# Final sum of the mixture of experts moved to TensorE, with accumulating stores onto a bias filled in early

## The chip, the cores and the metric

The kernel runs on one core of a Trainium2 chip. The metric is device time in microseconds (us). A profiled execution also has a span, from the first to the last recorded activity on the core, and its own time, which is a little more.

## What is computed

One step of a decoder layer for 512 prompt tokens and 32 sample tokens, 544 rows of width 1024, everything in 32-bit floats. An mLSTM branch and a pooling branch are mixed and projected, a layer norm follows, and then a mixture of experts (16 experts, two per token) and a second layer norm. The change is in the last line of this:

```python
gate = jnp.sum(jax.nn.one_hot(idx, N_EXPERTS) * wts[..., None], axis=1)       # two gates per token
h = jax.nn.silu(xt @ w_e_gate[e]) * (xt @ w_e_up[e]) * gate[:, e]             # for each expert e
x = LN(ALPHA * x + sum_e h_e @ w_e_down[e], ln2_g, ln2_b)                     # y = (s - mean) * rstd * g + b
```

The kernel computes each expert's output without its gate for the tokens routed to it. The last part applies the gates: s = ALPHA * x + gate_a * ya + gate_b * yb, with ya and yb the outputs of a token's two experts.

## The kernel before

All work is written out by hand for each engine, as one instruction stream each, with semaphores between them. The 544 rows are five tiles, four of 128 rows and one of 32 (`ROWS`). The stages are: transposing x, four heads of the mLSTM (h = 0 to 3) beside the wide projections, pooling, mixing, `w_out` with the first layer norm, the router, 16 experts, and the tail that this change is about.

**Loads.** Weights come as 1 MB chunks into three slots of `raw`, all issued by SyncE (SP) in one queue. `load_chunk(c)` waits until VectorE's subtraction (L431) has split the chunk that last used the slot. ScalarE makes the high part (L412) of a chunk and VectorE the low part (L431), since products are made as three float32r matmuls (L436 to L438). For each head h, SP loads the chunks 3h + 8 to 3h + 10, stores the head's states, waits for the store, and loads the state of the next head (`load_state`, L467).

**Second layer norm's parameters.** After the router's rows are stored, SP loads `ln2_g` into `lng` (L582) and `ln2_b` into `lnb` (L583), each broadcast to 128 partitions.

**Experts.** Expert outputs go from PSUM to `ys` (L985 by ScalarE, L1567 by VectorE) and by DMA to `y_slots` in HBM, 512 KB for each expert (L675 by GpSimd, the last one by SP at L598).

**The tail.** GpSimd (POOL) gathers each token's two expert rows from `y_slots` by indirect DMA (L713): five gathers into `ya` once the outputs of the experts before the last have landed, then five into `ybk` once the last has. `x1` already holds ALPHA * x (L973, ScalarE, during the experts). VectorE does the rest: `combine(i, 0)` (L1662) adds gate_a * ya for each tile; then for each tile `combine(i, 1)` (L1662 again) adds gate_b * yb, `stats` makes mean and variance (two L1674, L1676, L1677), `normal` subtracts the mean and multiplies with `lng` (L1681), and a last instruction multiplies with the reciprocal deviation and adds `lnb` (L1688). The combine of tile i + 1 stands between L1681 and L1688 of tile i, while GpSimd computes variance ** -0.5 (L726). SP stores each tile when L1688 has finished (L613). TensorE and ScalarE have nothing to do in the tail.

Of the kernel before, what the change touches and what calls it, by code (L numbers as in the profile page):

```python
# [5 lines left out]
ALU = mybir.AluOpType  # L6
ACT = mybir.ActivationFunctionType
F32 = mybir.dt.float32
# [7 lines left out]
P = 128  # L16
DM = 1024
SEQ, DB, DT = 512, 8, 4
NS = DB * DT
N = SEQ + NS  # L20
PT = SEQ // P
NT = PT + 1
# [11 lines left out]
ROWS = [P] * PT + [NS]  # L34
# [79 lines left out]
def build(nc, consts, x_prompt, x_sample, state_C, state_n, state_m, state_pool, w_in, b_gate, hn_gain, w_pool,  # L114
# [6 lines left out]
    def sem(name):  # L121
        sems[name] = ctx.enter_context(nc.semaphore(name))
        return sems[name]
# [30 lines left out]
    def lay(start, end, *items):  # L154

        out = []
        for name, shape, dt in items:
            out.append(place(name, shape, dt, start))
            start += size(shape, dt)
        assert start <= end, (items[-1][0], start - end)  # L160
        return out
# [28 lines left out]
    hmv = keep("hmv", [P, NT, 2])  # L190
    hve = keep("hve", [P, NT])
    hrs = keep("hrs", [P, NT])
# [4 lines left out]
    lst = keep("lst", [P, NT, 2, 6])  # L197
# [10 lines left out]
    end = cursor[0]  # L208
    assert end <= limit, (end - limit)
    r_moe = r1 + 31744  # L210
# [40 lines left out]
    x1, lng, lnb = lay(r_xt, XT_END, ("x1", [P, NT, DM], F32), ("lng", [P, DM], F32), ("lnb", [P, DM], F32))  # L251
# [36 lines left out]
    ya_rows = place("ya_rows", [P, PT, DM], F32, at_hi)  # L288
    ya_last = place("ya_last", [P, DM], F32, at_lo)
    ya = [ya_rows[:, i, :] for i in range(PT)] + [ya_last[:]]  # L290
    (ybk,) = lay(r_moe, end, ("ybk", [P, NT, DM], F32))
    yb_ = [ybk[:, i, :] for i in range(NT)]

    psum = ctx.enter_context(nc.psum_tensor("psum", [P, 8, 512], F32))
# [5 lines left out]
    def startup(i):  # L300

        return psum[:, 2 * (i % 4):2 * (i % 4) + 2, :]

    def narrow(j):
        return psum[:, 4 + j % 2, :]

    def halves(j):
# [3 lines left out]
    id_in, cst_in, par_in, gate_in, wg_in, nn_in, spn_in, wp_in, x1in, ln_in, wr_in = (  # L311
        sem(n) for n in (
            "id_in", "cst_in", "par_in", "gate_in", "wg_in", "nn_in", "spn_in", "wp_in", "x1in", "ln_in", "wr_in"))
# [3 lines left out]
    c_in, c_out, cp_out, outs, m_out, n_out, pool_out = (  # L317
        sem(n) for n in ("c_in", "c_out", "cp_out", "outs", "m_out", "n_out", "pool_out"))
# [30 lines left out]
    ya_in = [sem(f"ya_in{i}") for i in range(NT)]  # L349
    yb_in = [sem(f"yb_in{i}") for i in range(NT)]  # L350
    xal_ok, dve_tail = sem("xal_ok"), sem("dve_tail")
    fin_ok, v2_ok, r2_ok = (sem(n) for n in ("fin_ok", "v2_ok", "r2_ok"))


    def z_room(eng, j):
# [97 lines left out]
    def _(sp):  # L453
# [10 lines left out]
        def load_state(h):  # L464
            for dt in range(2):
                src = state_C[0][:, h, dt * P:(dt + 1) * P, :].rearrange("b p e -> p b e")
                sp.dma_start(cb[:, :, dt, 0:DH], src).then_inc(c_in, 16)  # L467
# [37 lines left out]
        for h in range(H):  # L505
            dense_chunk(3 * h + 8)
            if h == 0:
                with nc.allow_non_contiguous_dma(reason="one number for each head and sequence"):
                    sp.wait_ge(rows_dve, 1)
                    sp.dma_start(m_prompt[0].rearrange("o h -> h o"), mout[:, DB:DB + 1]).then_inc(m_out, 16)  # L510
                    sp.dma_start(m_sample[0].rearrange("b h -> h b"), mout[:, 0:DB]).then_inc(m_out, 16)
            store_prompt_state(h)
            dense_chunk(3 * h + 9)
            dense_chunk(3 * h + 10)
            if h < H - 1:
                store_sample_state(h)
                sp.wait_ge(c_out, 32 * h + 32)
                load_state(h + 1)
        sp.wait_ge(t_done, T_HEAD + 4 * T_PER_HEAD - 1)
        sp.dma_start(spn[:], state_pool[0].rearrange("b j c -> (b j) c")).then_inc(spn_in, 16)  # L520
        sp.dma_start(wp[:], w_pool[0].rearrange("g c e -> c g e")).then_inc(wp_in, 16)
# [58 lines left out]
        store_rows()  # L580
        sp.wait_ge(x1_out, 16 * NT)
        sp.dma_start(lng[:], ln2_g[0].partition_broadcast(P)).then_inc(ln_in, 16)  # L582
        sp.dma_start(lnb[:], ln2_b[0].partition_broadcast(P)).then_inc(ln_in, 16)  # L583
        sp.wait_ge(g_in[0], 16)
        with sp.Fori(1, NE - 1) as e:
            for j, (wt, half) in enumerate(((w_e_up, 0), (w_e_up, 1), (w_e_down, 0), (w_e_down, 1),
# [19 lines left out]
                    expert_chunk(m, 6 * j + (C_MOE + 96 + m - 6 + 1), wt, e, half)  # L606
            sp.nop()
        sp.nop()
        for i in range(NT):
            r = ROWS[i]  # L610
            sp.wait_ge(fin_ok, i + 1)
            dst = y_prompt[0, i * P:(i + 1) * P, :] if i < PT else y_sample.rearrange("b t d -> (b t) d")
            sp.dma_start(dst, x1[0:r, i, :]).then_inc(outs, 16)  # L613

        sp.wait_ge(outs, 16 * NT)
        sp.wait_ge(pool_out, 32)
        sp.wait_ge(n_out, 64)
# [6 lines left out]
    def _(pl):  # L624
# [85 lines left out]
        def gather_rows(a, buf, i):  # L710
            r = ROWS[i]
            idx = bass.IndirectOffsetOnAxis(ap=dest_i[0:r, a, i:i + 1].bitcast(U32), axis=0)
            pl.indirect_dma_start(buf[i][0:r], None, y_slots, idx).then_inc((ya_in, yb_in)[a][i], 16)  # L713
# [6 lines left out]
        pl.wait_ge(last_out, 16)  # L720
        for i in range(NT):
            gather_rows(1, yb_, i)
        for i in range(NT):
            r = ROWS[i]
            pl.wait_ge(v2_ok, i + 1)
            nc.gpsimd.tensor_tensor(hrs[0:r, i:i + 1], hve[0:r, i:i + 1], minus_half[0:r, 0:1],  # L726
                                    ALU.pow).then_inc(r2_ok, 1)


    @block.scalar  # L730
    def _(ac):
# [300 lines left out]
        with ac.If(extra > 0):  # L1032
# [11 lines left out]
                store_half(0)  # L1044
            ac.nop()
        ac.nop()


    @block.vector
    def _(ve_):  # L1050
# [605 lines left out]
        def step2(ins):  # L1656
            ve_.wait_ge(dve_tail, tail.mark(ins))

        def combine(i, a):
            r = ROWS[i]  # L1660
            ve_.wait_ge((ya_in, yb_in)[a][i], 16)
            return v.scalar_tensor_tensor(x1[0:r, i, :], (ya, yb_)[a][i][0:r], gates_ab[0:r, a, i:i + 1], x1[0:r, i, :],  # L1662
                                          ALU.mult, ALU.add)

        for i in range(NT):
            ve_.wait_ge(xal_ok, i + 1)
            last = combine(i, 0)
        step2(last)
        ve_.wait_ge(ln_in, 64)

        def stats(i):
            r = ROWS[i]
            for q in range(2):
                last = v.bn_stats(lst[0:r, i, q, :], x1[0:r, i, 512 * q:512 * q + 512])  # L1674
            step2(last)
            step2(v.bn_aggr(hmv[0:r, i, :], lst[0:r, i].rearrange("p q s -> p (q s)")))  # L1676
            v.tensor_scalar(hve[0:r, i:i + 1], hmv[0:r, i, 1:2], EPS, None, ALU.add).then_inc(v2_ok, 1)  # L1677

        def normal(i):
            r = ROWS[i]  # L1680
            last = v.scalar_tensor_tensor(x1[0:r, i, :], x1[0:r, i, :], hmv[0:r, i, 0:1], lng[0:r, :], ALU.subtract,  # L1681
                                          ALU.mult)
            if i < NT - 1:
                tail.mark(last)
                last = combine(i + 1, 1)
            step2(last)
            ve_.wait_ge(r2_ok, i + 1)
            v.scalar_tensor_tensor(x1[0:r, i, :], x1[0:r, i, :], hrs[0:r, i:i + 1], lnb[0:r, :], ALU.mult, ALU.add  # L1688
                                   ).then_inc(fin_ok, 1)

        step2(combine(0, 1))
        for i in range(NT):
            stats(i)
            normal(i)


    @block.tensor
    def _(pe):
# [485 lines left out]
            pe.nop()  # L2184
        pe.nop()


# [1 line left out]
_INS = ["x_prompt", "x_sample", "state_C", "state_n", "state_m", "state_pool", "w_in", "b_gate", "hn_gain", "w_pool",  # L2189
# [53 lines left out]
```

## Time and profile before

| | us |
|---|---|
| median of 3 runs | 968.62 (968.04 to 969.16) |
| the profiled execution's own time | 969.72 |
| its span | 968.3 |
| TensorE busy | 876.2 (90%) |
| VectorE busy | 599.3 (62%) |
| ScalarE busy | 385.6 (40%) |
| GpSimd busy | 92.5 (10%) |

Busy time of TensorE counts overlapping matmuls as one stretch, with modelled ends. The page also names the chain of work that ended last; for a change in the last 40 us only the end of that chain, in order of time, tells what is worth something.

### The profile page before, as it was taken

How to read it: one execution, taken by the hardware profiler on the slowest of the kernel's cores; microseconds unless marked ns; L12 is line 12 of the kernel's file. 1: busy time of each engine (PE TensorE's matmuls, PEld its weight loads, DVE VectorE, ACT ScalarE, POOL GpSimd, SP SyncE). 2: the span in 40 equal slices, each digit the busy share in tenths (PEclk: the TensorE clock that was granted, in tenths of full speed). 3: DMA queues.
4: the chain of work that ended last, by engine and by line, in shares of the span. 5: the costliest groups of instructions: out<-in, count | busy, mean ns of one | idle time of the engine just before them, and what ended most of it. 6: DMA issues, size and time to landing. Idle time of an engine off the chain costs nothing.

```text
span 968.3 us, 14553 instructions
## 1 busy us (share of the span) xinstructions
PE 876.2 (90%) x5981; PEld 790.2 (82%) x5981; DVE 599.3 (62%) x826; ACT 385.6 (40%) x401; POOL 92.5 (10%) x81
## 2 busy tenths in 40 slices
PE   6999999999999998999999998498889999999920
PEld 6989889888888987999999997377678888888810
DVE  4634453634646373132332455799999999999958
ACT  3522121141321332322222103466567777777600
POOL 3000000000000000101001011202111111110052
PEclk9989999999999999999999998599999999999975
DMA  9761161360533414223212831589799999999462
GB/s 286 237 239 45 55 217 45 98 218 18 190 110 106 145 56 133 79 65 113 92 62 72 327 123 53 194 307 346 298 372 412 420 415 407 414 413 390 197 228 92
DMA packets 79680, 195.78 MB, mean 202 GB/s; under 512 B 3906, under 2 KB 56858, under 8 KB 67337
## 3 DMA queue, kind: packets, MB, share of 16 engines
q1 hardware_dynamic: 72456, 169.40, 48.4%
q0 software_dynamic: 7168, 25.58, 6.9%
q8 instruction: 43, 0.70, 0.3%
q14 instruction: 13, 0.10, 0.0%
HBM read 167.65 MB, written 27.31 MB: 201 GB/s over the span
## 4 chain that ended last, share of the span: by engine, by line
PE 81%; DVE 11%; DMA 3%; ACT 3%; issue 1%; SPq 0%; POOL 0%; DVEq 0%
PE psum L436 24%; PE psum L438 23%; PE psum L437 23%; DVE split_lo L1395 3%; PE psum L1826 2%; PE psum L1845 2%; PE psum L1836 1%; DVE onehot L1490 1%; DVE last_lo L1395 1%; DMA xg<-x_rows,idx_i 1%; PE psum L2071 1%; PE psum L1874 1%; ACT split_hi L412 1%; PE psum L2025 1%; DMA xn<-in_x_prompt_dram 1%
## 5 line engine op out<-in xcount | busy, mean ns | idle before, releaser
L436 PE MATMUL psum<-x_hi,split_lo 128*128 128x272 f32 x704 | 211.0, 300 | 12.5 <-ACT ht L820 8.3
L437 PE MATMUL psum<-x_lo,split_hi 128*128 128x272 f32 x704 | 203.8, 289 | 0.0
L438 PE MATMUL psum<-x_hi,split_hi 128*128 128x272 f32 x704 | 203.7, 289 | 0.0
L1395 DVE TENSOR_TENSOR split_lo<-raw,split_hi 128x2048 fp32r<-128x2048 f32 x72 | 163.3, 2287 | 11.9 <-ACT split_hi L951 10.2
L431 DVE TENSOR_TENSOR split_lo<-raw,split_hi 128x2048 fp32r<-128x2048 f32 x35 | 80.1, 2290 | 128.5 <-ACT split_hi L412 128.4
L951 ACT CAST split_hi<-raw 128x2048 fp32r<-128x2048 f32 x72 | 137.7, 1914 | 53.3 <-PE psum L438 48.1
L436 PEld LDWEIGHTS psum<-x_hi,split_lo 128*128 128x128 f32 x704 | 134.3, 191 | 17.6 <-ACT ht L820 9.3
L437 PEld LDWEIGHTS psum<-x_lo,split_hi 128*128 128x128 f32 x704 | 134.5, 191 | 1.5 <-issue 1.0
L438 PEld LDWEIGHTS psum<-x_hi,split_hi 128*128 128x128 f32 x704 | 134.2, 191 | 0.0
L436 PE MATMUL psum<-split_hi,xgl 128*128 128x512 f32 x188 | 76.3, 406 | 0.5 <-DVE xgl L1551 0.5
L438 PE MATMUL psum<-split_hi,xgh 128*128 128x512 f32 x188 | 74.4, 396 | 0.0
L437 PE MATMUL psum<-split_lo,xgh 128*128 128x512 f32 x188 | 74.4, 396 | 0.0
L412 ACT CAST split_hi<-raw 128x2048 fp32r<-128x2048 f32 x35 | 66.7, 1905 | 3.9 <-DMA raw<-in_w_in_dram 3.9
L1395 DVE TENSOR_TENSOR last_lo<-raw,last_hi 128x2048 fp32r<-128x2048 f32 x24 | 54.9, 2287 | 4.5 <-ACT last_hi L951 4.5
L951 ACT CAST last_hi<-raw 128x2048 fp32r<-128x2048 f32 x24 | 45.8, 1909 | 12.9 <-PE psum L438 12.9
L436 PE MATMUL psum<-split_hi,x_lo 128*128 128x256 f32 x160 | 47.3, 295 | 0.0
L438 PE MATMUL psum<-split_hi,x_hi 128*128 128x256 f32 x160 | 45.7, 286 | 0.0
L437 PE MATMUL psum<-split_lo,x_hi 128*128 128x256 f32 x160 | 45.7, 285 | 0.0
L669 POOL DMA_INDIRECT xg<-x_rows,idx_i x16 | 31.0, 1937 | 131.1 <-PE psum L2071 80.3
L438 PEld LDWEIGHTS psum<-split_hi,xgh 128*128 128x128 f32 x188 | 36.0, 192 | 7.9
L436 PEld LDWEIGHTS psum<-split_hi,xgl 128*128 128x128 f32 x188 | 36.1, 192 | 7.8 <-issue 0.7
L437 PEld LDWEIGHTS psum<-split_lo,xgh 128*128 128x128 f32 x188 | 36.2, 193 | 7.2
(373 smaller groups left out, 1758.9 us busy)
## 6 DMA issues: line engine op xcount, KB each, us to landing
raw<-in_w_e_gate_dram SPq DMA_DIRECT2D x32, 1024.0 KB, 8.3
raw<-in_w_e_up_dram SPq DMA_DIRECT2D x32, 1024.0 KB, 7.9
raw<-in_w_e_down_dram SPq DMA_DIRECT2D x32, 1024.0 KB, 7.6
raw<-in_w_in_dram SPq DMA_DIRECT2D x26, 1024.0 KB, 6.0
cb<-in_state_C_dram SPq DMA_DIRECT2D x8, 1024.0 KB, 8.2
out_dram<-cb SPq DMA_DIRECT2D x8, 1024.0 KB, 6.2
y_slots<-ys POOLq DMA_DIRECT2D x15, 512.0 KB, 8.0
y_slots<-x_hi POOLq DMA_DIRECT2D x2, 2048.0 KB, 12.1
```

Source lines behind the costliest of these rows:

```text
L412: nc.scalar.copy(split_hi[:, c % SPLIT_SLOTS, :], raw[:, c % RAW_SLOTS, :]).then_inc(w_hi, 1)
L431: nc.vector.tensor_tensor(split_lo[:, slot, :], raw[:, c % RAW_SLOTS, :], split_hi[:, slot, :].bitcast(F32), ALU.subtract).then_inc(w_lo, 1)
L436: nc.tensor.matmul(out, a_lo, b_hi, start=first, stop=False)
L437: nc.tensor.matmul(out, a_hi, b_lo, start=False, stop=False)
L438: return nc.tensor.matmul(out, a_hi, b_hi, start=False, stop=last)
L669: pl.indirect_dma_start(xg[e % 2][:], None, x1_rows, idx).then_inc(g_in[e % 2], 16)
L951: nc.scalar.copy(hi, raw2[:, n % MOE_SLOTS, :]).then_inc(w_hi, 1)
L1395: v.tensor_tensor(lo, raw2[:, n % MOE_SLOTS, :], hi.bitcast(F32), ALU.subtract).then_inc(w_lo, 1)
L1490: last = v.tensor_tensor(onehot[:, i, 0:e1 - e0], bc(const("slot"), 1, [P, e1 - e0, P]), bc(tmp_r[:, i, e0:e1], 2, [P, e1 - e0, P]), ALU.i ...
L1826: last = mm(narrow(j)[:, 0:SEQ - i * P], kt[:, c, i * P:i * P + P], qt[:, c, i * P:SEQ], start=c == 0, stop=c == 1)
L1836: last = mm(psum[:, state_bank(c), 0:VW], kw[:, i, whole(c)], ve[:, i, :], start=i == 0, stop=i == PT - 1)
L1845: last = mm(narrow(j)[:, 0:VW], pb[:, at:at + P], ve[:, i, :], start=i == 0, stop=i == t)
```

## The change

The second combine, VectorE's last instruction per tile and SP's store are replaced.

- ScalarE, after its last expert output, writes five 128x128 diagonal matrices with gate_b on the diagonal (`diag`, placed behind `ybk`).
- TensorE adds into PSUM, two banks for each tile: identity times `x1` (`sum_start`, when gate_a * ya has been added to it) and diagonal times `ybk` (`sum_end`, when the gather has landed). Each is two plain float32 matmuls of 512 columns, 20 in all. The order is: starts of tiles 0 to 3, ends of tiles 0 to 3, start and end of tile 4, which uses the banks of tile 0.
- VectorE keeps the first combine, takes the statistics from PSUM, and writes (sum - mean) * `lng` to `x1` (`centred`). It no longer waits for GpSimd's power. Order: stats(0), centred(0), stats(1), centred(1), ...
- ScalarE multiplies `x1` with the reciprocal deviation, one activation per tile.
- GpSimd, after each power, waits for that activation and issues the tile's store itself, as a DMA that adds to what is in HBM.
- What it adds to is `ln2_b`: SP fills the whole outputs with it, five HBM-to-HBM DMAs with a broadcast source, behind `load_state(2)` in head 1. `ln2_b` is no longer loaded into `lnb`.

```diff
@@ sync engine, in the loop over heads
+            if h == 1:
+                for i in range(PT):
+                    sp.dma_start(y_prompt[0, i * P:(i + 1) * P, :], ln2_b[0].partition_broadcast(P)).then_inc(bias_out, 16)
+                sp.dma_start(y_sample.rearrange("b t d -> (b t) d"), ln2_b[0].partition_broadcast(NS)
+                             ).then_inc(bias_out, 16)
@@
-        sp.dma_start(lnb[:], ln2_b[0].partition_broadcast(P)).then_inc(ln_in, 16)
@@
-        for i in range(NT):
-            r = ROWS[i]
-            sp.wait_ge(fin_ok, i + 1)
-            dst = y_prompt[0, i * P:(i + 1) * P, :] if i < PT else y_sample.rearrange("b t d -> (b t) d")
-            sp.dma_start(dst, x1[0:r, i, :]).then_inc(outs, 16)
@@ gpsimd
+        pl.wait_ge(bias_out, 16 * NT)
         for i in range(NT):
             r = ROWS[i]
             pl.wait_ge(v2_ok, i + 1)
             nc.gpsimd.tensor_tensor(hrs[0:r, i:i + 1], hve[0:r, i:i + 1], minus_half[0:r, 0:1],
                                     ALU.pow).then_inc(r2_ok, 1)
+            pl.wait_ge(n2_ok, i + 1)
+            dst = y_prompt[0, i * P:(i + 1) * P, :] if i < PT else y_sample.rearrange("b t d -> (b t) d")
+            pl.dma_start(dst, x1[0:r, i, :], accum_op=ALU.add).then_inc(outs, 16)
@@ scalar
+        for i in range(NT):
+            r = ROWS[i]
+            nc.scalar.activation(diag[0:r, i, 0:r], const("ident", r)[:, 0:r], ACT.Copy, scale=gates_ab[0:r, 1, i:i + 1]
+                                 ).then_inc(dg_ok, 1)
+        for i in range(NT):
+            r = ROWS[i]
+            ac.wait_ge(pf_ok, i + 1)
+            ac.wait_ge(r2_ok, i + 1)
+            nc.scalar.activation(x1[0:r, i, :], x1[0:r, i, :], ACT.Copy, scale=hrs[0:r, i:i + 1]).then_inc(n2_ok, 1)
@@ vector
         def stats(i):
             r = ROWS[i]
+            ve_.wait_ge(pc_ok, i + 1)
             for q in range(2):
-                last = v.bn_stats(lst[0:r, i, q, :], x1[0:r, i, 512 * q:512 * q + 512])
+                last = v.bn_stats(lst[0:r, i, q, :], summed(i)[0:r, q, :])
@@
+        def centred(i):
+            r = ROWS[i]
+            v.scalar_tensor_tensor(x1[0:r, i, :], summed(i)[0:r].rearrange("p b n -> p (b n)"), hmv[0:r, i, 0:1],
+                                   lng[0:r, :], ALU.subtract, ALU.mult).then_inc(pf_ok, 1)
+
+        stats(0)
+        for i in range(NT):
+            centred(i)
             if i < NT - 1:
-                tail.mark(last)
-                last = combine(i + 1, 1)
-            step2(last)
-            ve_.wait_ge(r2_ok, i + 1)
-            v.scalar_tensor_tensor(x1[0:r, i, :], x1[0:r, i, :], hrs[0:r, i:i + 1], lnb[0:r, :], ALU.mult, ALU.add
-                                   ).then_inc(fin_ok, 1)
+                stats(i + 1)
@@ tensor
+        def sum_start(i):
+            r = ROWS[i]
+            pe.wait_ge(xa2_ok, i + 1)
+            if i >= PT:
+                pe.wait_ge(pf_ok, i - PT + 1)
+            for q in range(2):
+                mm(summed(i)[0:r, q, :], ident[0:r, 0:r], x1[0:r, i, q * 512:q * 512 + 512], start=True, stop=False)
+
+        def sum_end(i):
+            r = ROWS[i]
+            pe.wait_ge(dg_ok, i + 1)
+            pe.wait_ge(yb_in[i], 16)
+            for q in range(2):
+                last = mm(summed(i)[0:r, q, :], diag[0:r, i, 0:r], yb_[i][0:r, q * 512:q * 512 + 512], start=False,
+                          stop=True)
+            last.then_inc(pc_ok, 1)
+
+        pe.wait_ge(dg_ok, 1)
+        for i in range(PT):
+            sum_start(i)
+        for i in range(PT):
+            sum_end(i)
+        sum_start(PT)
+        sum_end(PT)
```

## Rows read from the trace of the kernel before

**Rows 1.** Page, chain that ended last, shares of the span by engine.
```profile
PE 81%; DVE 11%; DMA 3%; ACT 3%; issue 1%; SPq 0%; POOL 0%; DVEq 0%
```
**Rows 2.** Chain of waits, the end: start us, length us, what.
```profile
927.21 6.72 DMA y_slots<-ys
...
934.18 4.71 DMA ybk<-y_slots,dest_i
...
939.01 1.30 DVE x L1662
...
945.76 1.21 DVE lst L1674 x2
...
947.39 1.19 DVE x L1681
948.58 1.21 DVE x L1662
...
951.10 1.21 DVE lst L1674 x2
...
965.05 1.27 DVE x L1688
```
**Rows 3.** One line's answer, last line: the stores of L613.
```profile
DMA to landing us min/median/max: 1.9/2.6/2.6
```
**Rows 4.** Instructions in order of time, tail: start us, length us, engine, line, operation.
```profile
926.44 0.59 ACT L985 COPY ys<-psum 128x512 f32<-128x512 f32 x1 [6.55 <-PE psum L438]
...
927.76 1.28 DVE L1662 SCALAR_TENSOR_TENSOR x<-ya_rows,gates_ab,x 128x1024 f32<-128x1024 f32 x1 [0.63 <-DMA ya_rows<-y_slots,dest_i]
...
930.97 2.58 DVE L1662 SCALAR_TENSOR_TENSOR x<-ya_rows,gates_ab,x 128x1024 f32<-128x1024 f32 x2 [1.92 <-DMA ya_rows<-y_slots,dest_i]
...
934.81 1.29 DVE L1662 SCALAR_TENSOR_TENSOR x<-ya_rows,gates_ab,x 128x1024 f32<-128x1024 f32 x1 [1.27 <-DMA ya_rows<-y_slots,dest_i]
```
**Rows 5.** Chain of waits, head 0: plain float32 matmuls, 128x512 (two matmuls are four records).
```profile
79.65 1.91 PE psum L1826 x4
```
**Rows 6.** Stretches: us, busy us (count) by engine, PEclk, DMA share, GB/s.
```profile
622.00:623.00 1.00, 0.79 (x2) 0.70 (x3) 1.00 (x1) 0.15 (x1) 0.70 (x2) 0.50 0.88 360
626.00:627.00 1.00, 1.00 (x4) 0.78 (x4) 0.00 (x0) 0.00 (x0) 0.00 (x0) 0.70 0.96 401
880.00:900.00 20.00, 20.00 (x96) 16.74 (x95) 19.16 (x13) 15.29 (x12) 0.56 (x1) 1.00 1.00 393
930.00:931.00 1.00, 0.00 (x0) 0.00 (x0) 0.03 (x1) 0.00 (x0) 0.00 (x0) 0.69 0.98 397
950.00:968.00 18.00, 0.00 (x0) 0.00 (x0) 15.53 (x21) 0.00 (x0) 4.55 (x3) 0.50 0.24 95
```
**Rows 7.** By line: ns min/median/max, first and last start (ScalarE, GpSimd).
```profile
L973 ACT ACTIVATE x<-x x5: 1038/1039/1039, 609.5 to 613.3; 128x1024 f32<-128x1024 f32 x4, 32x1024 f32<-32x1024 f32 x1
L806 ACT ACTIVATE pb<-pb x16: 293/297/315, 73.2 to 264.7; 128x128 f32<-128x128 f32 x16
L726 POOL TENSOR_TENSOR hrs<-hve,cst x5: 1515/1520/1537, 942.1 to 963.4; 128x1 f32<-128x1 f32 x4, 32x1 f32<-32x1 f32 x1
L675 POOL DMA_DIRECT2D y_slots<-ys x15: 533/583/607, 666.3 to 920.1; - x15
DMA to landing us min/median/max: 2.9/8.0/9.1
```
**Rows 8.** Instructions in order of time, GpSimd's indirect gathers, tail.
```profile
938.46 0.94 POOL L713 DMA_INDIRECT ybk<-y_slots,dest_i  x1 [0.30 <-issue]
```
**Rows 9.** By tile x: ns min/median/max of a VectorE operation with a PSUM source.
```profile
L1423 DVE SCALAR_TENSOR_TENSOR x<-x,psum x4: 954/955/955, 555.5 to 585.0; 128x768 f32<-128x768 f32 x4
```
**Rows 10.** Instructions in order of time, heads 1 and 2: SP, ScalarE.
```profile
203.52 1.66 SPq L459 DMA_DIRECT2D raw<-in_w_in_dram  x1
...
257.08 1.90 ACT L412 CAST split_hi<-raw 128x2048 fp32r<-128x2048 f32 x1
```
**Rows 11.** Stretch of heads 1 and 2, columns as in rows 6.
```profile
219.00:239.00 20.00, 20.00 (x167) 17.98 (x166) 8.13 (x26) 3.46 (x6) 0.00 (x0) 1.00 0.00 1
```

More of the change, by code:

```diff
@@ L290, in build @@
     ya = [ya_rows[:, i, :] for i in range(PT)] + [ya_last[:]]
-    (ybk,) = lay(r_moe, end, ("ybk", [P, NT, DM], F32))
+    ybk, diag = lay(r_moe, end, ("ybk", [P, NT, DM], F32), ("diag", [P, NT, P], F32))
     yb_ = [ybk[:, i, :] for i in range(NT)]
@@ L302, in startup, with summed @@
         return psum[:, 2 * (i % 4):2 * (i % 4) + 2, :]
+    def summed(i):
+        return psum[:, 2 * (i % PT):2 * (i % PT) + 2, :]
     def narrow(j):
@@ L351, in build @@
     xal_ok, dve_tail = sem("xal_ok"), sem("dve_tail")
-    fin_ok, v2_ok, r2_ok = (sem(n) for n in ("fin_ok", "v2_ok", "r2_ok"))
+    dg_ok, xa2_ok, pc_ok, pf_ok = (sem(n) for n in ("dg_ok", "xa2_ok", "pc_ok", "pf_ok"))
+    v2_ok, r2_ok, n2_ok, bias_out = (sem(n) for n in ("v2_ok", "r2_ok", "n2_ok", "bias_out"))
     def z_room(eng, j):
@@ L1657, in step2 @@
             ve_.wait_ge(dve_tail, tail.mark(ins))
-        def combine(i, a):
+        for i in range(NT):
             r = ROWS[i]
[L1661 to L1665, printed above, removed]
             ve_.wait_ge(xal_ok, i + 1)
-            last = combine(i, 0)
-        step2(last)
-        ve_.wait_ge(ln_in, 64)
+            ve_.wait_ge(ya_in[i], 16)
+            v.scalar_tensor_tensor(x1[0:r, i, :], ya[i][0:r], gates_ab[0:r, 0, i:i + 1], x1[0:r, i, :], ALU.mult, ALU.add
+                                   ).then_inc(xa2_ok, 1)
+        ve_.wait_ge(ln_in, 48)
         def stats(i):
             r = ROWS[i]
+            ve_.wait_ge(pc_ok, i + 1)
             for q in range(2):
-                last = v.bn_stats(lst[0:r, i, q, :], x1[0:r, i, 512 * q:512 * q + 512])
+                last = v.bn_stats(lst[0:r, i, q, :], summed(i)[0:r, q, :])
             step2(last)
@@ L1677, in stats @@
             v.tensor_scalar(hve[0:r, i:i + 1], hmv[0:r, i, 1:2], EPS, None, ALU.add).then_inc(v2_ok, 1)
-        def normal(i):
+        def centred(i):
             r = ROWS[i]
-            last = v.scalar_tensor_tensor(x1[0:r, i, :], x1[0:r, i, :], hmv[0:r, i, 0:1], lng[0:r, :], ALU.subtract,
-                                          ALU.mult)
-            if i < NT - 1:
-                tail.mark(last)
-                last = combine(i + 1, 1)
-            step2(last)
-            ve_.wait_ge(r2_ok, i + 1)
-            v.scalar_tensor_tensor(x1[0:r, i, :], x1[0:r, i, :], hrs[0:r, i:i + 1], lnb[0:r, :], ALU.mult, ALU.add
-                                   ).then_inc(fin_ok, 1)
[L1691 to L1694, printed above, removed]
+            v.scalar_tensor_tensor(x1[0:r, i, :], summed(i)[0:r].rearrange("p b n -> p (b n)"), hmv[0:r, i, 0:1],
+                                   lng[0:r, :], ALU.subtract, ALU.mult).then_inc(pf_ok, 1)
+        stats(0)
+        for i in range(NT):
+            centred(i)
+            if i < NT - 1:
+                stats(i + 1)
     @block.tensor
```

## The prediction

> **What bounds the kernel now.** I read the page's chain shares first, then the end of the chain in order of time, then the stretches of the tail. Over the whole span the chain is TensorE's for 81% [rows 1], and nothing of that is touched. The change lives in the last 40 us, and there the chain is another one [rows 2]: the last expert's store (927.21, 6.72 us), the gather of tile 0's second expert rows (934.18, 4.71 us), and from 939.01 to 966.32 VectorE without a break. Its period is 5.34 us per tile (945.76 to 951.10). In it stand statistics 1.63 (945.76 to 947.39), centring 1.19 (to 948.58), the next combine and L1688. The last L1688 starts at 965.05 and takes 1.27; the store of the 32-row tile then lands in 1.9 [rows 3], which gives 966.3 + 0.1 + 1.9 = 968.3, the span. TensorE stands still all that time at half its clock, and ScalarE does nothing [rows 6]. So what VectorE is rid of is worth its full length until something else is later.
>
> **VectorE.** It loses five second combines (1.2 to 1.3 each) and five L1688 (1.27), its two longest pieces of four. What is left per tile is 1.63 + 1.19 = 2.82; I take 2.85 with a semaphore wait. The power no longer stands in its stream. Its operations now read PSUM; a row with a PSUM source has 955 ns for 768 elements, 1.24 ns each [rows 9], and the combine from SBUF 1.28 us for 1024, 1.25 each [rows 4]. So I charge nothing. The Trainium skill says otherwise ("VectorE: DVE Perf Modes", the section on the TRN2 errata: the table gives 120 fixed cycles from PSUM and 58 from SBUF, at 0.96 GHz). By it each PSUM read would be 65 ns dearer; the trace does not show that in this pair of rows, and by the page my time would be 0.2 us later.
>
> **TensorE, the new work.** Twenty plain float32 matmuls of 512 columns. Two such are 1.91 us at the full clock [rows 5]; at the half clock I double it to 3.82, an estimate from that row and PEclk 0.50. Each tile needs a pair for its start and a pair for its end. Starts wait for VectorE's first combines, which end at 929.05, 932.3, 933.55 and 936.1 [rows 4]. The diagonals cost ScalarE 5 x 0.30 = 1.5 us [rows 7] after its last copy ends at 927.03 [rows 4], so until 928.6; combine 0 hides them, with 0.4 us to spare, and only the first is waited for.
> The clock decides how long the starts take. Before, the last matmul ended at 926.4 and PEclk for 930 to 931 is 0.69, so the drop to 1.2 GHz came near 930.5; it came back at about 626.7 (PEclk 0.70 in that microsecond) after TensorE had worked from 622.2 on, 4.5 us [rows 6]. I take both over: start 0 runs 929.1 to 931.1, start 1 from 932.3 at half clock to 936.1, start 2 from there, the clock returns near 937, so start 2 ends at 938.6 and start 3 at 940.5. Then the ends: tile 0's gather has landed at 938.9 [rows 2], so end 0 is 940.5 to 942.4. The others follow at 1.9 (944.3, 946.2, 948.1, and 952 for tile 4); their gathers are long down (the fourth is issued at 938.46 [rows 8], plus 4.71 [rows 2] is 943.2). Bounds of the first end: 940.8 with a full clock throughout (938.9 + 1.91), 947.6 at half clock throughout (932.3 + 4 x 3.82).
>
> **After the sum.** stats(0) runs 942.5 to 944.15, then VectorE gives a variance every 2.85 us. GpSimd gets more: per tile now power 1.52, then it waits for ScalarE's scaling 1.04 [rows 7], then issues the store, then the next power. Queued behind that wait is the next tile's power, and ScalarE and the store wait for it. That is a serial loop of 1.52 + 1.04 + the issue + some 0.25 for semaphores. An accumulating store is not in the trace. The nearest issue is GpSimd's plain DMA to HBM, 0.58 [rows 7]; the dear one is its indirect gather, 0.94 and 0.30 of idle [rows 8], 1.24. I take 0.58, since the addresses are direct: 3.4 us per tile (4.05 by the other). It is longer than VectorE's 2.85, so GpSimd's loop is the pacer. SP's old issue was 0.3 to 0.4 off VectorE's path; that it goes gives nothing. First issue: 944.2 + 1.55 + 1.1 = 946.9. Fifth issue: 946.9 + 4 x 3.4 = 960.5. The last centring of VectorE (956.8) is inside that.
> Landing: GpSimd's 512 KB writes took at least 2.9 [rows 7], a plain 128 KB store by SP 1.9 [rows 3]. An accumulating one also reads HBM. Lower bound 1.9; upper bound by the slowest GpSimd write, 9.1 (under load) [rows 7]. I take 2.9, as the tail is not loaded. End 963.4, against 968.3: minus 4.9.
>
> The transfers queue behind one another only if one takes more than the loop's 3.4. Plain, 512 KB at the 393 GB/s of a full stretch [rows 6] is 1.3 us, 2.6 times less. The Trainium skill speaks against the change here ("Collectives: The Full Stack", "Stop ④ — SDMA + CCE: where bytes move and the add happens", and the fold count part behind it): the adding itself is free, but two reads per write halve the rate, measured 1.93. No row here shows it. By that page a 512 KB store would move in 2.6 us, still under 3.4, and only the last, quarter-size one would land 0.3 later.
>
> **The fills in head 1.** Five HBM-to-HBM DMAs, 2.2 MB written, in SP's queue behind `load_state(2)` and ahead of the chunk issued at 203.52 [rows 10]. SP's dearest issue there is 1.66, so at most 8.3 us; the data is 5.7 us at 393 GB/s [rows 6]; allow twice, 11.4. Cover: from 219 to 239 the DMA share is 0.00 [rows 11], so everything then in flight had landed by 219, and the chunk's cast is at 257.08 [rows 10] (the three casts between are for older chunks). That is 38 us of cover for at most 20, and head 2's state is read in the late 230s by TensorE, which was busy 20.00 of 20.00 us in that stretch. Zero. Without cover it would be those microseconds, one for one. The dropped load of `lnb` (512 KB after the router) had landed 300 us before use; zero too, on either side.
>
> **Sum.** VectorE's stream gives 5 x 2.5 = 12.5; back go 3.5 (TensorE's first end, 942.4 against the combine's 939.0), about 2.2 because the loop's four periods are 3.4 and not 2.85, and some 2 for the power, scaling and dearer store behind the last tile. Span 963.4. The profiled execution has 969.72 for a span of 968.3, and the median run is 968.62, 1.1 lower than it; taking 4.9 off the median gives 963.7.
>
> **The rivals.**
> *Quicker.* The clock stays up, the first end is at 940.8, 1.6 earlier, and the store lands in 1.9, 1.0 earlier: 961.1. For it: start 0 falls into the gap in which the clock had still been up. Against: TensorE works only 2 of the 5 us before 932.
> *TensorE never gets its clock back (the other side).* It gives 1.2 GHz for all pairs. Starts and ends then follow at 3.82: first end 947.6, ends 951.4, 955.2, 959.1, and tile 4's start and end 966.7. Behind it stand 1.7 of statistics, 1.6 power, 1.1 scaling, 2.9 store: span 974.0, or 974.3. It decides once the last end is later than 961.0. For it: PEclk is 0.50 through 940 to 968 [rows 6], and work comes in bits. Against: from 932.3 on there is no gap, and 4.5 us without one were enough at 622.
> *Accumulating stores are slow (slower too).* Each 512 KB takes T; the end is 946.9 + 1.3 + 4.25 T, which passes 968.3 at T = 4.7, 3.6 times the plain 1.3. At T = 5.5 it is 971.6, or 971.9. Between 3.4 and 4.7 it eats the gain. For it: no row of such a transfer. Against: 2.1 MB in 13.6 us is only 155 GB/s.
> *Dear issue.* The loop is 4.05: fifth issue 963.1, end 966.0, or 966.3.
>
> **How the numbers follow.** Forecast 0.57, dear issue 0.10 and quick 0.11 are all faster: 0.78. Never the full clock 0.06 and slow stores 0.11, of which 0.02 ends within 0.2% (1.9 us, about what this measurement can tell from no change); fills on the path or another mishap 0.05, 0.03 of it within 0.2% and 0.02 slower. So faster 0.78, same 0.05, slower 0.17. Range: 960.9 (the quick case) to 968.4, which leaves out most of the slower cases.
>
> **What would show it.** Right: VectorE's tiles at 2.85 plus idle, the first statistics at 942.5, its idle ended by TensorE; GpSimd's power every 3.4 with idle ended by ScalarE; nothing different before 926. Wrong: PEclk 0.50 throughout with TensorE ends 3.8 apart; a store that lands after more than 4.7; an end of head 1 or 2 that is later than before.

## The result, and the profile after

The changed kernel takes 958.67 us (median of 4 runs, 955.95 to 960.38) against 968.76 for the kernel before on the same chip (4 runs, 968.04 to 969.16): 0.9894 of its time [0.9867, 0.9922]. The forecast was 963.7, with a range from 960.9 to 968.4. The direction was right; the gain is 10 us where 4.9 were forecast, and the time lies below the range. The profiled execution took 959.97 us for a span of 958.8.

The page of the kernel after, shares of the chain that ended last [rows 1]:

```profile
PE 83%; DVE 9%; ACT 3%; DMA 2%; issue 2%; POOL 1%; DVEq 0%; SPq 0%; ACTq 0%; POOLq 0%
```

Its chain of waits, the end: start us, length us, what [rows 2]:

```profile
928.18 8.89 PE psum L2200 x16
937.07 1.86 PE psum L2207 x4
...
939.02 1.31 DVE lst L1687 x2
...
940.75 1.20 DVE x L1694
941.98 1.16 ACT x L1062
...
943.43 0.99 POOL out_dram L734
944.43 0.61 POOL hrs L730
...
945.12 1.16 ACT x L1062
946.27 0.29 issue
946.57 0.90 POOL out_dram L734
947.47 0.60 POOL hrs L730
...
955.59 0.82 POOL out_dram L734
```

VectorE's unbroken stream has gone from the chain. In its place stands the loop that the prediction named: GpSimd's power, ScalarE's scaling (L1062), GpSimd's store. Its period is 945.12 to 948.15, 3.03 us, where 3.4 was forecast, and it started 3.5 us sooner than forecast (first store issued at 943.43, not 946.9). The first line names the starts and not the gather as what tile 0's end waited for; the two came together, the gather landing 4.6 us after its issue at 932.27, at 936.9, and the end beginning at 936.96.

The kernel after in order of time, the tail: start us, length us, engine, line, operation, idle before it and what ended it [rows 4, 8]:

```profile
925.22 0.58 ACT L992 COPY ys<-psum 128x512 f32<-128x512 f32 x1 [6.55 <-PE psum L443]
...
932.27 0.95 POOL L716 DMA_INDIRECT ybk<-y_slots,dest_i  x1 [3.49 <-DMA y_slots<-ys]
...
936.96 1.96 PE L2207 MATMUL psum<-ybk,diag 128*128 128x512 f32 x4
...
940.67 1.27 DVE L1694 SCALAR_TENSOR_TENSOR x<-psum,hmv,lng 128x1024 f32<-128x1024 f32 x1
940.90 0.56 POOL L730 TENSOR_TENSOR hrs<-hve,cst 128x1 f32<-128x1 f32 x1 [1.77 <-DVE hve L1690]
...
944.14 0.88 POOL L730 TENSOR_TENSOR hrs<-hve,cst 128x1 f32<-128x1 f32 x1
```

The first power takes 0.56 us; before, every one took 1.52 to 1.54 [rows 7]. The four later ones are recorded with 0.85 to 0.88, but each begins some 0.27 us before the end of the store's issue ahead of it and adds 0.60 to it, as the chain has it.

ScalarE's last copy of expert rows is the last event that both kernels have alike, so from here on a tail is measured from its start to the end of the span. Before it is 926.44 [rows 4] to 968.3, 41.9 us; after it is 925.22 to 958.8, 33.6. The change is worth 8.3 us there, by one trace of each. The other 1.2 us of the two spans' difference is older than the change's work; e1 is about it.

Stretches of the kernel after: us, busy us (count) of TensorE, weight loads, VectorE, ScalarE, GpSimd, then TensorE's granted clock, DMA share, GB/s [rows 6]:

```profile
930.00:932.00 2.00, 2.00 (x3) 0.84 (x3) 1.65 (x2) 0.00 (x0) 0.00 (x0) 0.50 0.86 330
932.00:934.00 2.00, 2.00 (x5) 0.81 (x4) 0.74 (x2) 0.00 (x0) 1.43 (x2) 0.79 0.17 47
934.00:936.00 2.00, 2.00 (x6) 0.86 (x5) 1.85 (x2) 0.00 (x0) 1.69 (x2) 1.00 0.75 250
949.00:952.00 3.00, 0.00 (x0) 0.00 (x0) 2.90 (x8) 1.15 (x2) 1.47 (x2) 0.65 1.09 171
```

The granted clock fell to 1.2 GHz at 929.4 and was back at 2.4 GHz at 932.8, some four microseconds earlier than the 937 of the forecast; until it rose, TensorE had been busy without a gap since 928.18. In the last row VectorE is at 2.90 of 3.00 us: its own period (2.83) is nearly as long as that of GpSimd's loop.

The store's line and the scaling's, by line: ns min/median/max, first and last start [rows 3, 7]:

```profile
L734 POOL DMA_DIRECT2D out_dram<-x x5: 817/878/992, 943.4 to 955.6; - x5
...
DMA to landing us min/median/max: 3.1/5.5/5.9
...
L1062 ACT ACTIVATE x<-x,hrs x5: 1147/1147/1147, 942.0 to 954.2; 128x1024 f32<-128x1024 f32 x4, 32x1024 f32<-32x1024 f32 x1
```

An adding store costs GpSimd 0.88 us to issue (a plain one 0.58 [rows 7]) and lands in 5.5; only the landing of the last, quarter-size one is on the path: 955.59 to the end of the span, 3.2.

The fills. SP in order of time, heads 1 and 2, of the kernel after [rows 10]:

```profile
176.49 0.38 SPq L476 DMA_DIRECT2D out_dram<-cp  x1
...
200.92 3.71 SPq L526 DMA_DIRECT2D out_dram<-in_ln_b_dram  x4
204.68 0.60 SPq L527 DMA_DIRECT2D out_dram<-in_ln_b_dram  x1
205.32 0.58 SPq L464 DMA_DIRECT2D raw<-in_w_in_dram  x1
...
238.28 0.39 SPq L476 DMA_DIRECT2D out_dram<-cp  x1
```

and the same two marks of the kernel before:

```profile
177.72 0.38 SPq L471 DMA_DIRECT2D out_dram<-cp  x1
...
239.50 0.38 SPq L471 DMA_DIRECT2D out_dram<-cp  x1
```

61.79 us with the fills between the marks, 61.78 without: they cost nothing, as forecast. All twelve traces, of which the kernel before and e6 have no fills, have 61.78 to 61.80 here.

### The profile page after: what moved, and what is told of

It reads as the page before. It is cut to its first block, busy times and chain, and to the rows that moved or that the text cites. A ratio compares the mean times of both kernels' runs of the same rounds, so it can differ in the third digit from the quotient of the medians.

```text
span 958.8 us, 14645 instructions
## 1 busy us (share of the span) xinstructions
PE 895.3 (93%) x6021; PEld 796.7 (83%) x6021; DVE 586.8 (61%) x816; ACT 392.5 (41%) x411; POOL 92.1 (10%) x86
## 4 chain that ended last, share of the span: by engine, by line
PE 83%; DVE 9%; ACT 3%; DMA 2%; issue 2%; POOL 1%; DVEq 0%; SPq 0%; ACTq 0%; POOLq 0%
PE psum L441 24%; PE psum L443 23%; PE psum L442 23%; DVE split_lo L1411 3%; PE psum L1833 2%; PE psum L1852 2%; PE psum L1843 1%; DVE onehot L1506 1%; DMA xg<-x_rows,idx_i 1%; DVE last_lo L1411 1%; PE psum L2078 1%; PE psum L1881 1%; PE psum L2200 1%; ACT split_hi L417 1%; PE psum L2032 1%
## 5 line engine op out<-in xcount | busy, mean ns | idle before, releaser
L1411 DVE TENSOR_TENSOR split_lo<-raw,split_hi 128x2048 fp32r<-128x2048 f32 x72 | 163.4, 2288 | 12.2 <-ACT split_hi L958 10.5
L441 PE MATMUL psum<-split_hi,htl 128*128 128x512 f32 x96 | 38.7, 403 | 3.7 <-DVE split_lo L1411 2.3
```

What stands on the lines that cost most here:

```text
L441: nc.tensor.matmul(out, a_lo, b_hi, start=first, stop=False)
L1411: v.tensor_tensor(lo, raw2[:, n % MOE_SLOTS, :], hi.bitcast(F32), ALU.subtract).then_inc(w_lo, 1)
```

## The experiments

Each edit is against the changed kernel, but e5's, which is against the kernel before. Each ratio is to runs of the kernel before that were taken with it; their medians go from 967.08 to 968.89. The last two columns are from one trace each: the tail from the last copy, and the part of it from the first statistics on, both to the end of the span; the difference between them is the wait for the last expert's rows and the sum of tile 0. Between the kernel before and the change it stays (13.9 and 13.8); the gain is behind the first statistics.

| kernel | median us | ratio to before | tail | of it behind the first statistics |
|---|---|---|---|---|
| before | 968.76 | 1 | 41.9 | 28.0 |
| the change | 958.67 | 0.9894 [0.9867, 0.9922] | 33.6 | 19.8 |
| e1, the change again | 960.91 | 0.9936 [0.991, 0.9961] | 33.7 | 20.2 |
| e2, centring from SBUF | 960.01 | 0.9921 [0.9894, 0.9947] | 35.6 | 20.2 |
| e3, plain stores | 961.24 | 0.9921 [0.9891, 0.9951] | 31.65 | 17.9 |
| e4, burst of adding stores | 971.24 (one run) | | 46.4 | 31.4 |
| e5, stores half alone | 965.91 | 0.999 [0.9967, 1.0013] | 39.3 | 26.4 |
| e6, sum half alone | 961.54 | 0.9938 [0.9917, 0.9959] | 36.6 | 22.4 |
| e7, TensorE kept busy | 961.72 | 0.9941 [0.9919, 0.9963] | 33.5 | 19.7 |
| e8, last store plain | 958.93 | 0.9911 [0.9877, 0.9944] | 33.4 | 19.5 |
| e9, last two plain | 961.68 | 0.9925 [0.99, 0.995] | 32.7 | 18.7 |
| e10, burst of plain stores | 963.31 (one run) | | 37.8 | 23.4 |

**e1, the changed kernel once more, unedited.**

> The changed kernel once more, for a second trace and more times. The four times of it so far lie 4.4 us apart (955.95 to 960.38), those of the kernel before 1.1. Theory A: the tail now contains TensorE work whose clock falls and returns at moments that differ from run to run; then this trace, if its time differs by 2 us or more from 959.97, shows a different end of the first sum relative to the last expert's matmul (925.2 to 938.9 in the first trace, 13.7 us), or another PEclk between 928 and 934. Theory B: the spread comes from the last transfers; then the first sum stands at 13.7 us and the store's landing (3.1 to 5.9) differs. Theory C: it is upstream of the tail; then the last expert's matmul is not at 925.2. Median expected 957 to 960 in all cases.

Measured 960.91 (958.49 to 963.95, 6 runs). The tail is the same (33.7 and 33.6), yet the last copy starts at 923.70 here and at 925.22 in the first trace; over all twelve traces it starts anywhere from 921.66 (e5) to 929.45 (e3). So theory C holds: runs differ by several microseconds in work ahead of the tail. SP's marks in the twelve traces show where: the store of head 0's state starts anywhere from 111.3 to 115.5, from head 2's to head 3's it is 62.0 us or, in e3, e7, e8 and e9, 63.6, and from the store of the router's rows (558 to 565) to the last expert's store 363.8 to 366.0 (365.9 in the first trace of the change, 364.1 in this one). The first of these lies ahead of every edit; what causes any of them was not tried. The first batch was a low sample of the changed kernel; its ten unedited runs together have the median 959.8, which is 7.5 and 8.9 below the two medians of the kernel before that were taken with them, in line with the tail's 8.3. The spread is also why verdicts below are read from tails and not from medians, which can't tell one microsecond.

**e2, the centring reads `x1` and not PSUM** (so it leaves the second expert's rows out of the centring).

```diff
-            v.scalar_tensor_tensor(x1[0:r, i, :], summed(i)[0:r]..., hmv[0:r, i, 0:1],
+            v.scalar_tensor_tensor(x1[0:r, i, :], x1[0:r, i, :], hmv[0:r, i, 0:1],
```

> Centring reads x1 from SBUF and not the sum from PSUM, so the second expert's share is left out of the output; the order and the waits are those of the changed kernel. GpSimd's power took 1.52 us before and 0.56 to 0.88 in the changed kernel. Theory A: it is slow while VectorE reads two tensors from SBUF. Then the power is back at 1.4 to 1.6 us, GpSimd's loop goes from 3.0 to about 3.9 us per tile, and the span grows by some 4 us. Theory B: it is faster for another reason (GpSimd has just issued a DMA, or has less to do before): then it stays at 0.56 to 0.88 and the span within 1 us of the changed kernel.

In order of time, the first tile:

```profile
940.19 1.27 DVE L1694 SCALAR_TENSOR_TENSOR x<-x,hmv,lng 128x1024 f32<-128x1024 f32 x1
940.42 1.47 POOL L730 TENSOR_TENSOR hrs<-hve,cst 128x1 f32<-128x1 f32 x1 [3.19 <-DVE hve L1690]
```

The same power that took 0.56 us beside a centring with a PSUM source takes 1.47 beside one whose two tensors are both in SBUF, and it ends 0.43 us after VectorE's instruction. So theory A is right about the power, and wrong about what it costs. The later powers are as long as in the change:

```profile
944.15 0.88 POOL L730 TENSOR_TENSOR hrs<-hve,cst 128x1 f32<-128x1 f32 x1
```

By the time GpSimd has issued its store the centring is all but over (943.02 to 944.29 here); so the loop is not longer (four periods take 12.16 us in both kernels), and only the first store comes 0.5 us later after the first statistics. The rest of this tail's 2.0 us more lies ahead of the statistics, in the gather and the starts.

**e3, the stores don't add** (the output lacks the bias).

```diff
-            pl.dma_start(dst, x1[0:r, i, :], accum_op=ALU.add).then_inc(outs, 16)
+            pl.dma_start(dst, x1[0:r, i, :]).then_inc(outs, 16)
```

> The five final stores of the changed kernel without the addition, so ln2_b is overwritten and left out of the output. Theory A (GpSimd's loop paces, the transfer is only at the very end): the loop stays at 3.0 us, the landing falls from 3.1 to 5.9 us to about 2.9, DMA share in the tail from 1.0 to about 0.4, the span is 0 to 0.6 us shorter. Theory B (the adding transfers fill the DMA engines and set the end): the span is 1.5 us or more shorter. The issue on GpSimd, 0.82 to 0.99 us in the changed kernel against 0.58 for its plain 512 KB stores before, shows whether adding makes the issue dearer.

By line, and one stretch with a store in it, columns as above:

```profile
L734 POOL DMA_DIRECT2D out_dram<-x x5: 537/576/632, 947.6 to 958.9; - x5
...
DMA to landing us min/median/max: 2.2/2.9/3.2
```
```profile
952.00:955.00 3.00, 0.60 (x2) 0.00 (x0) 2.93 (x6) 1.32 (x2) 1.14 (x2) 1.00 0.48 201
```

The issue is 0.30 us shorter and the landing 0.9 to 2.7 shorter; the period falls from 3.03 to 2.83, and VectorE then sets it. The four periods are 0.9 us shorter in all, the last landing 1.0. The DMA share of the 3 us is 0.48, against 1.09 in the changed kernel at 171 GB/s. Adding costs the tail 1.9 us: theory B's size, half of it from the loop that theory A took to stay. TensorE's clock stayed at 2.4 GHz in this trace through all the starts, without any edit to that end, and the first end still began 11.70 us after the last copy (11.74 in the change).

**e4 and e10, all five stores behind the last scaling**, adding in e4, plain in e10 (which lacks the bias).

```diff
-            pl.wait_ge(n2_ok, i + 1)
+        pl.wait_ge(n2_ok, NT)
+        for i in range(NT):
+            r = ROWS[i]
```

> GpSimd makes all five powers first and issues the five adding stores back to back after the last scaling, to measure the rate of an adding 512 KB transfer by itself. In the changed kernel the DMA share is 1.03 to 1.09 at 166 to 187 GB/s with one store every 3.0 us. Theory A: the engines are at their limit there: then the stores land 2.8 to 3.0 us apart and the span is about 14 us from the first issue, some 968 to 970. Theory B: they are busy by accounting only: the stores land at the pace of the issues, 1.2 us apart, and the span ends near 962 to 963.

> The burst of e4 without the addition (ln2_b is overwritten): five stores issued back to back after the last scaling. There, 2.2 MB took from 954.3 to 970.0, 15.7 us. Theory: a plain 512 KB takes 1.3 to 1.4 us of the DMA engines, the issue 0.58 and a gap of up to 0.3, so the transfers still set the pace: 4.25 x 1.35 + 1.5 = 7.2 us from first issue to the end, half of the adding burst. Rival: GpSimd's stores to HBM are slow whether they add or not; then it is 12 us or more.

The issues in order of time and the stretches of e4, then the issues of e10:

```profile
954.31 4.51 POOL L736 DMA_DIRECT2D out_dram<-x  x5 [2.08 <-ACT x L1064]
```
```profile
961.00:964.00 3.00, 0.00 (x0) 0.00 (x0) 0.00 (x0) 0.00 (x0) 0.00 (x0) 0.50 1.00 186
964.00:967.00 3.00, 0.00 (x0) 0.00 (x0) 0.00 (x0) 0.00 (x0) 0.00 (x0) 0.50 1.04 206
```
```profile
954.35 2.73 POOL L736 DMA_DIRECT2D out_dram<-x  x5 [2.06 <-ACT x L1064]
```

The 2.2 MB take 15.7 us adding (954.31 to 970.0) and 7.75 plain (954.35 to 962.1). With nothing else running, the 16 engines are full at 186 to 206 GB/s. If the last store's own time is taken off (3.2 us in the change, 2.2 in e3), the four of 512 KB ahead of it take 3.1 us each adding and 1.4 plain, an estimate that counts the start of the burst in; at the 201 to 209 GB/s that e4 has from 963 to 967 it would be 2.6 for 512 KB. The loop's period is 3.03, and the change has a DMA share of 1.01 to 1.09 from 945 to 958: its stores run nearly back to back. That a faster loop would have met them was not tried. The Trainium skill ("Collectives: The Full Stack", "The bandwidth ceiling: the fold count and why AG ≠ RS ≠ AR") gives 1.93, measured for a collective of four ranks, as the ratio of the rate of the step that copies to that of the step that adds. Here the two bursts as a whole give 2.03, each of the four stores 2.2, and the full stretches 1.9 (e10 has 389 to 401 GB/s from 957 to 961): the traces agree.

**e5 and e6, each half alone.** e5 keeps both combines on VectorE, and bias fills and adding stores; VectorE's last instruction is then a multiplication alone. e6 keeps TensorE's sum and gives VectorE its last instruction, and SP the plain stores.

```diff
+            v.tensor_scalar(x1[0:r, i, :], x1[0:r, i, :], hrs[0:r, i:i + 1], None, ALU.mult).then_inc(fin_ok, 1)
```
```diff
+            v.scalar_tensor_tensor(x1[0:r, i, :], x1[0:r, i, :], hrs[0:r, i:i + 1], lnb[0:r, :], ALU.mult, ALU.add
+                                   ).then_inc(n2_ok, 1)
```

> Only one half of the change: the kernel before with the outputs filled with ln2_b in head 1, VectorE's last instruction a multiplication with the reciprocal deviation alone, and adding stores issued by GpSimd. Tail = from ScalarE's last copy of an expert's output to the end of the span: 41.9 us before (926.44 to 968.3), 33.6 and 33.7 in two traces of the changed kernel. Theory: the gain of 8.2 us is VectorE's share of the sum and scaling; this half alone saves at most what the one-operand multiplication is shorter than 1.28 us, five times, and costs 1.5 us at the end for the dearer issue and landing: tail 39.5 if a multiplication takes 0.6 to 0.7, 43.3 if it takes 1.28. GpSimd's power stays at 1.5, as VectorE reads two SBUF tensors beside it. Rival: the early fill and the store are what pays; then the tail is 37 or less.

> The other half alone: TensorE makes the second sum, VectorE still multiplies with the reciprocal deviation and adds ln2_b (1.28 us), SP stores plainly, no fill. Theory: first sum 13.7 us after ScalarE's last copy, then VectorE's five tiles at 1.63 + 1.19 + 1.28 = 4.1, 0.6 of wait for the last power, 1.9 landing: tail 37.0, that is 4.9 of the 8.2 us. GpSimd's power 0.56 to 0.6, since centring reads PSUM. Rival: TensorE's sum alone gives little, because its first end comes 1 to 4 us after the old first combine: tail 39 to 41.

VectorE and a store of e5, then VectorE and GpSimd of e6, in order of time:

```profile
938.73 0.75 DVE L1692 TENSOR_SCALAR x<-x,hrs 128x1024 f32<-128x1024 f32 x1
...
958.23 0.82 POOL L731 DMA_DIRECT2D out_dram<-x  x1 [1.14 <-DVE x L1692]
```
```profile
939.06 1.28 DVE L1687 SCALAR_TENSOR_TENSOR x<-psum,hmv,lng 128x1024 f32<-128x1024 f32 x1
939.23 0.56 POOL L731 TENSOR_TENSOR hrs<-hve,cst 128x1 f32<-128x1 f32 x1 [2.11 <-DVE hve L1683]
...
941.90 1.28 DVE L1694 SCALAR_TENSOR_TENSOR x<-x,hrs,lnb 128x1024 f32<-128x1024 f32 x1
942.06 1.54 POOL L731 TENSOR_TENSOR hrs<-hve,cst 128x1 f32<-128x1 f32 x1 [2.27 <-DVE hve L1683]
```

The sum alone takes the tail from 41.9 to 36.6 (period 4.04 per tile), the stores alone to 39.3 (period 4.80), both together to 33.6: 5.3, 2.6 and 8.3, so the halves nearly add up, to 7.9. The stores alone can't be told from the kernel before in its median. e6 shows the two lengths of the power in one trace: 0.56 beside the PSUM source, 1.54 beside `x` and `lnb`. The Trainium skill has a rule for this that the prediction overlooked ("SBUF — State Buffer", "Who interferes with whom"): a VectorE instruction with two SBUF inputs contends with a GpSimd instruction that reads SBUF. e2 and e6 agree, with 1.47 and 1.54 against 0.56; it is the power that waits, as VectorE's instruction keeps its 1.27 and 1.28.

**e7, TensorE kept busy through the starts.**

```diff
+        fill(12)
         pe.wait_ge(dg_ok, 1)
         for i in range(PT):
             sum_start(i)
+            fill((3, 0, 2, 0)[i])
```

`fill(n)` issues n matmuls of 512 columns of weights into a PSUM bank that nothing reads.

> The changed kernel with 17 filler matmuls (float32r, 512 columns, 0.23 us each, into a bank that is free) in TensorE's waits between the last expert and the sums, 12 before the first start, 3 and 2 between starts, so that its clock does not fall. The forecast had put 3.5 us on the half clock. Theory A: by the traces the first end waits for tile 0's gather anyway (the starts are through at 936.96 and the gather landed at about the same time): PEclk stays 1.00 and the tail is 33.0 to 33.7. Theory B: the clock costs what the eight halves of the starts lose, 2 us or more: tail 31.7 or less.

Stretches, columns as above, and the first end:

```profile
930.00:932.00 2.00, 1.90 (x7) 0.98 (x6) 1.01 (x2) 0.54 (x3) 1.48 (x1) 1.00 0.96 320
932.00:934.00 2.00, 2.00 (x7) 1.13 (x7) 1.55 (x2) 0.00 (x0) 0.00 (x0) 1.00 1.00 397
```
```profile
934.97 0.96 POOL L716 DMA_INDIRECT ybk<-y_slots,dest_i  x1 [3.50 <-DMA y_slots<-ys]
...
939.82 7.36 PE L2207 MATMUL psum<-ybk,diag 128*128 128x512 f32 x16
```

The clock stays at 2.4 GHz, and the tail is 33.5. The first end starts 11.73 us after the last copy (928.09), where the change itself has 11.74. In both, tile 0's gather and the last start are there together: here the gather lands 4.7 us after its issue, at 939.7, and start 3, which waited until 937.67 for VectorE's first combine of tile 3, is through at 939.7 too. So theory A holds: the half clock of the change costs nothing in that trace.

**e8 and e9, the last store, or the last two, plain and by SP**, from VectorE's former last instruction.

```diff
+        v.scalar_tensor_tensor(x1[0:NS, PT, :], x1[0:NS, PT, :], hrs[0:NS, PT:NT], lnb[0:NS, :], ALU.mult, ALU.add
+                               ).then_inc(fin_ok, 1)
...
+        sp.wait_ge(fin_ok, 1)
+        sp.dma_start(y_sample.rearrange("b t d -> (b t) d"), x1[0:NS, PT, :]).then_inc(s_out, 16)
```

> The changed kernel with tile 4 (the 32 sample rows) taken out of the adding stores: VectorE scales it and adds ln2_b (1.27 us, after its last centring), SP stores it plainly; its output is not filled early and ln2_b is loaded to SBUF again. Theory: GpSimd's loop has four turns and not five, the end is tile 3's adding store (issued 12.9 us after the first sum, landing 4.5 to 5.5 later) or tile 4's plain one (power at 14.7, scaled at 16.1, landed at 18.1): tail 31.8 to 32.3 against 33.6. Rival: the adding transfers are the limit (2.9 us per 512 KB of the loop's 3.0), and tile 3 lands after 18.6 whatever comes behind it: tail 32.5 to 33.6, no clear gain.

> Tiles 3 and 4 are taken out of the adding stores: VectorE scales them and adds ln2_b, SP stores them plainly. Theory: with tile 4 alone taken out nothing was gained, because tile 3's adding store, 5.6 to 5.9 us from issue to landing, ended last; adding transfers take 2.9 us per 512 KB and the loop issues one every 3.0. Now the third adding store is issued 10.7 us after the first sum and has landed by 16.5, so that VectorE sets the end: variance of tile 4 at 13.1 after the first sum, scaling 3, centring 4, scaling 4 until 16.8, landed at 18.8 against 19.9. Tail (from ScalarE's last copy of an expert's output) 32.5 against 33.5 to 33.7. Rival: something other than the adding transfers held tile 3; then the tail stays at 33.4 or more.

DMA issues of e8, KB each and us to landing, then those of e9:

```profile
out_dram<-x POOLq DMA_DIRECT2D x4, 512.0 KB, 5.6
...
out_dram<-x SPq DMA_DIRECT2D x1, 128.0 KB, 3.0
```
```profile
out_dram<-x POOLq DMA_DIRECT2D x3, 512.0 KB, 5.5
out_dram<-x SPq DMA_DIRECT2D x1, 512.0 KB, 3.1
out_dram<-x SPq DMA_DIRECT2D x1, 128.0 KB, 2.0
```

In e8 the plain store is issued at 955.93 and needs 3.0 us instead of 1.9 [rows 3], beside tile 3's adding store, issued at 953.07, which lands about 958.6: the tail is 33.4, no better than 33.6 by more than 0.2. With tile 3's store plain too the last one lands in 2.0, and the tail is 32.7, 0.9 below the change. That is the shortest tail of a complete kernel here, but 961.68 against 958.93 and 960.91 in medians says nothing of it, so a better kernel is not shown.

## Why the prediction fell short

**The mechanism was right.** VectorE ceases to be the bound; the loop power, scaling, store on GpSimd and ScalarE is the pacer; nothing stems from the fills; the diagonals cost nothing. "I charge nothing" for the PSUM sources holds: the centring takes 1.27 us from PSUM and 1.27 from SBUF (e2). The lag from the first sum to the first issue is 4.5 us (938.93 to 943.43), as forecast, but by luck: the power was 1.0 us shorter than the forecast's 1.52, and ScalarE then waited for the centring, which ended at 941.94, a wait that the forecast does not have; scaling and its hand-over to the store took 0.35 us longer.

**Three terms of the sum were mis-sized.** In the tail:

| term | forecast | measured | us |
|---|---|---|---|
| first sum ends after the last copy | 16.0 | 13.7 | -2.3 |
| four periods of the loop | 13.6 | 12.2 | -1.4 |
| last landing | 2.9 | 3.2 | +0.3 |

Together 3.4: the change is worth 8.3 where 4.9 were forecast.

*The first sum.* The step that failed is "the clock returns near 937, so start 2 ends at 938.6 and start 3 at 940.5". That put the first end 1.6 behind its gather (940.5 against 938.9); in the trace the starts were through as the gather landed, at 936.9 to 937.0. Another 0.7 is a gather issued 7.05 us after the copy and not 7.74; over the changed kernel and its edits this runs from 6.6 to 7.7, so it is spread and no effect of the change.

The forecast has the clock at 1.2 GHz for 6.5 us, from 930.5 to 937; it was there for 3.4, from 929.4 to 932.8. It let the 4.5 us taken from 622 begin with start 1, at 932.3, behind a gap. But tile 1's first combine was through at 930.48, start 1 followed start 0 without a gap, and the clock was back 4.6 us after start 0 had begun; in e1 it was 3.4 us, in e2 5.7, so one stretch could not give the number. (At 622 TensorE had also worked from 619 to 621, which the forecast left out.) The bound given, 940.8 at a full clock, was the better value: e3 and e7 show that a full clock gives no more than the change has.

The clock is not free in every run: in e2 it was at 1.2 GHz for 6.8 us, the starts took 9.96 us and not 8.89 and held the first end up by 1.2, the gather having landed at 935.3 and the end beginning at 936.56. In e4, e6, e8, e9 and e10, with 3.4 us at 1.2 GHz each, the first end waits for its gather; in e1 it waits 0.5 us for start 3, which itself could begin only when VectorE's first combine of tile 3 was through.

*The loop.* Forecast 1.52 + 1.04 + 0.58 + 0.25 = 3.4; measured 0.60 behind the issue + 1.15 + 0.88 + 0.37 = 3.0. The step that failed is the power at 1.52: it had that beside L1681, with both tensors in SBUF [rows 7]. The change takes that neighbour away in two ways. For the first power it is the PSUM source of the centring, as e2 shows. For those of the loop their place is enough: they start behind a store's issue, when the centring is over or nearly so, and e2 has the same length there with the centring from SBUF. The three other terms were each too low, by 0.5 us together. Had the power been the only error, four periods would have been off by 3.7 us and not 1.4; the rival of the dear issue was half right for its reason (0.88, between 0.58 and 1.24), and wrong in its time.

*The slow adding store.* By the prediction each 512 KB would have to take T = 4.7 us before the change loses; e4 gives 3.1, or 2.6 at the rate of its full stretches, about the loop's period or less. The prediction asked whether the landing time, 5.5 us, would be the danger ("a store that lands after more than 4.7"): it does land later than that, and nothing follows. Landing time (5.5) is not the time for which one store holds the engines (3.1 or less); e4 measures the second. Adding still costs 1.9 us against plain stores (e3), in the issue and in the last landing.

**The rest of the miss is no part of the change.** 958.67 lies 5.0 below the forecast: 3.4 in the tail, 1.1 because the first four runs were low ones (the ten unedited runs have 959.8), and 0.5 that nothing here explains. What spreads the work ahead of the tail was not tried and stays open. The marks of the two kernels differ by 1.2 us at 177 already (and at 114), before anything of the change has run, so it is neither the tail nor the fills.

**The rivals.** The quick case (961.1) was the nearest, and right that the first end is not held up by the clock, though the clock did fall, for 3.4 us; its landing of 1.9 did not come (3.2). TensorE at 1.2 GHz throughout did not occur in any trace.

## What to carry to other kernels

When an engine is relieved, price the successor's loop with its operations as they will stand beside their new neighbours: a tiny GpSimd operation may have been long only because of what VectorE read beside it, and in a new order it may start when that neighbour is gone. For a queue of transfers the cost is what one occupies, and a burst of them measures it; the time to landing matters for the last one alone. Where the spread of earlier work is as large as the effect, compare stretches from the last common event, and keep medians for the sum.

## What the runs showed of the hardware

- GpSimd's 128x1 power: 0.53 to 0.57 us beside a VectorE operation that reads PSUM (e3, e4), 1.47 to 1.54 beside one that reads two SBUF tensors (e2, e6). Behind an adding store's issue it is recorded with 0.85 to 0.88, 0.60 of it behind that issue. The first layer norm of the changed kernel, where VectorE reads SBUF, keeps the old value:

```profile
L661 POOL TENSOR_TENSOR hrs<-hve,cst x5: 1509/1515/1525, 557.1 to 597.0; 128x1 f32<-128x1 f32 x4, 32x1 f32<-32x1 f32 x1
```

- A 128x1024 float32 multiplication by a per-row scalar takes VectorE 0.75 us (e5), where the same with a second tensor takes 1.28.
- ScalarE's activation with a scale per row takes 1.147 us for 1024 elements, with a fixed one 1.039 [rows 7].
- TensorE's clock in the tail, with work from the first start on: at 1.2 GHz for 3.4 us in the change, e1, e4, e6, e8, e9 and e10, for 6.8 in e2, and not at all in e3, though TensorE's instructions are the same in all of these.
- VectorE's statistics of 512 elements take 0.682 us from PSUM and 0.678 from SBUF, centring 1.275 from PSUM and 1.276 from SBUF.
- A DMA that adds: issue 0.88 against 0.58 us, landing 5.5 against 2.9 for 512 KB (e3), and about twice the time of the engines (e4, e10). A plain store of 128 KB queued beside one needs 3.0 instead of 1.9 us (e8).
